# Weight splits in halves of 1024 columns instead of whole units of 2048, in a chain of two transformer models on one core

## The reference

```
first_block:  for i in 0, 1:
                  h = h + mixer_i(rmsnorm(h))        # 0: dilated windows, 24 heads; 1: block attention, 16 heads
                  h = h + square(relu(rmsnorm(h) @ w1)) @ w2            # w1 1024 x 4096, w2 4096 x 1024
second_block: h = layer_norm(16 meta tokens + x)                        # 272 rows
              for i in 0, 1:
                  u = h @ w_in                                          # 1024 x 3840
                  y_attn = sliding_window_attention(u) @ w_attn_proj
                  y_conv = silu(layer_norm(depthwise conv of 31 taps(u))) @ w_conv_proj
                  h = layer_norm(ALPHA*h + (sigmoid(ga)*y_attn + sigmoid(gc)*y_conv) @ w_out)
                  f = swiglu(h)  (i = 0)   or   mixture of 8 experts, 2 per token, each 1024 x 1408  (i = 1)
                  h = layer_norm(ALPHA*h + f)
```

## Time and profile before

| what | value |
|---|---|
| three executions | 1688.42, 1688.47, 1685.88 us; median 1688.42 |
| profiled execution | span 1685.1 us from first to last instruction; its own time is not listed apart |
| TensorE's granted clock | 0.987 of full speed on average |
| busy: PE, DVE, ACT, POOL | 97%, 73%, 57%, 19% of the span |

### The profile page before, as it was taken

The page is one execution under the profiler, slowest core; times in us unless marked ns, Lnnn a source line. Parts: engine busy times, 40 slices in busy tenths (PEclk is TensorE's granted clock), DMA queues, the critical chain, the costliest instruction groups (busy, mean ns, idle before and its releaser), DMA issues.

```text
span 1685.1 us, 27573 instructions
## 1 busy us (share of the span) xinstructions
PE 1639.9 (97%) x11042; PEld 1488.0 (88%) x11042; DVE 1238.1 (73%) x1760; ACT 966.9 (57%) x1374; POOL 322.1 (19%) x320
## 2 busy tenths in 40 slices
PE   8999999999989999999999999999899999999997
PEld 6988888898878889998899999999888888888886
DVE  6555666656557656898775554799788899888897
ACT  5556575446656734555454433555547777776775
POOL 2333553123325502143020001131020000000000
PEclk9999999999989999999999999999989999999999
DMA  7632455555234554543335454543328888888993
GB/s 295 230 110 91 150 191 188 183 204 185 101 124 177 195 183 181 184 150 119 134 124 200 175 175 175 167 151 128 149 75 322 343 338 344 332 336 331 352 346 127
DMA packets 50197, 339.76 MB, mean 202 GB/s; under 512 B 5575, under 2 KB 7839, under 8 KB 10351
## 3 DMA queue, kind: packets, MB, share of 16 engines
q1 hardware_dynamic: 47344, 328.79, 53.1%
q0 software_dynamic: 2720, 9.13, 1.7%
HBM read 336.76 MB, written 1.13 MB: 201 GB/s over the span
## 4 chain that ended last, share of the span: by engine, by line
PE 87%; DVE 6%; ACT 4%; issue 2%; POOL 1%; DMA 1%; SPq 0%; DVEq 0%; ACTq 0%; POOLq 0%
PE bank L509 12%; PE bank L483 8%; PE bank L485 8%; PE bank L484 8%; PE bank L507 7%; PE bank L927 5%; PE bank L928 5%; PE bank L929 5%; PE bank L640 3%; PE bank L642 3%; PE bank L641 3%; PE bank L960 2%; PE bank L959 2%; PE bank L958 2%; ACT wh L1165 1%
## 5 line engine op out<-in xcount | busy, mean ns | idle before, releaser
L1640 DVE TENSOR_TENSOR wl<-stg,wh 128x2048 fp32r<-128x2048 f32 x310 | 712.9, 2303 | 237.5 <-ACT wh L1165 235.3
L1165 ACT ACTIVATE wh<-stg 128x2048 fp32r<-128x2048 f32 x310 | 592.5, 1912 | 203.8 <-PE bank L929 85.2
L483 PE MATMUL bank<-xx,wh 128*128 128x272 f32 (+1 forms) x810 | 235.1, 290 | 1.1 <-DVE xx L2062 1.0
L485 PE MATMUL bank<-xx,wl 128*128 128x272 f32 (+1 forms) x810 | 232.5, 287 | 0.0
L484 PE MATMUL bank<-xx,wh 128*128 128x272 f32 (+1 forms) x810 | 232.3, 287 | 0.0
L509 PE MATMUL bank<-xx,wh 128*128 128x512 f32 x448 | 161.1, 398 | 0.0
L483 PEld LDWEIGHTS bank<-xx,wh 128*128 128x128 f32 x810 | 152.4, 188 | 3.0 <-issue 1.9
L484 PEld LDWEIGHTS bank<-xx,wh 128*128 128x128 f32 x810 | 153.6, 190 | 0.0
L485 PEld LDWEIGHTS bank<-xx,wl 128*128 128x128 f32 x810 | 152.4, 188 | 0.0
L509 PE MATMUL bank<-H,wh 128*128 128x512 f32 x434 | 151.3, 390 | 0.0
L927 PE MATMUL bank<-wh,GH 128*128 128x512 f32 (+3 forms) x400 | 147.6, 369 | 0.0
(11 more groups left out here) (366 smaller groups left out, 3526.8 us busy)
## 6 DMA issues: line engine op xcount, KB each, us to landing
stg<-in_w SPq DMA_DIRECT2D x310, 1024.0 KB, 4.8
BT<-bias_scratch POOLq DMA_DIRECT2D x3, 1024.0 KB, 11.4
BT<-bias_scratch POOLq DMA_DIRECT2D x1, 2048.0 KB, 13.0
BB<-bias_scratch POOLq DMA_DIRECT2D x2, 1024.0 KB, 6.5
res<-in_x SPq DMA_DIRECT2D x1, 1024.0 KB, 5.7
stg<-in_w SPq DMA_DIRECT2D x2, 512.0 KB, 6.8
BB<-bias_scratch POOLq DMA_DIRECT2D x2, 512.0 KB, 7.1
out<-res SPq DMA_DIRECT2D x4, 256.0 KB, 3.3
```

What stands on the lines that cost most here:

```text
L483: pe.matmul(out, wh, xh(kt), start=kt == 0, stop=False)
L485: ins = pe.matmul(out, wl, xh(kt), start=False, stop=kt == KT - 1)
L1165: act.activation(WH[u % NW][:, :], stg[u % NS][:, :], ACT.Copy).then_inc(*m.inc("w_high", u))
L1640: vec.tensor_tensor(WL[u % NW][:, :], stg[u % NS][:, :], WH[u % NW][:, :].bitcast(F32), ALU.subtract).then_inc(*m.inc("w_low_v", u))
```

## The change

Every split is made in halves v = 0 ... 621, of 1024 columns each, with an event of its own on each of the three engines: TensorE waits for the half it enters (`half_ready`) and gives back half by half, ScalarE's split of half v waits for TensorE's half v-6, VectorE's for ScalarE's half v. `enter(v)` puts down splits up to half v+5, at each half. The DMAs stay units of 1 MB and wait for the second half of unit u-4. `go_on` makes up for halves, and where a `one_ahead` stood outside the start it now adds one half. TensorE's matmuls and their order are the same.

```diff
+HU = UT // 2
+        def half_of(bufs, v):
+            return bufs[v // 2 % len(bufs)][:, v % 2 * HALF:(v % 2 + 1) * HALF]
...
-            def unit_ready(u):
-                w.wait_ge(*m.of("w_high", u))
-                w.wait_ge(*m.of("w_low_v", u))
+            def half_ready(v):
+                w.wait_ge(*m.of("w_high", v))
+                w.wait_ge(*m.of("w_low_v", v))
...
             def enter(self, u):
-                while self.made < min(u + NW, N_UNITS) and not self.held:
+                while self.made < min(u + 2 * NW, 2 * N_UNITS) and not self.held:
                     self.split(self.made)
                     self.made += 1
...
             def go_on(self):
                 self.held = False
-                self.enter((self.at - 1) // UT)
+                self.enter((self.at - 1) // HU)
...
-            def split(u):
-                w.wait_ge(*m.of(f"w_in{u % NS}", u))
-                if u >= NW:
-                    w.wait_ge(*m.of("group" if u - NW < EXPERT_UNIT else arm[0], ("unit", u - NW)))
-                act.activation(WH[u % NW][:, :], stg[u % NS][:, :], ACT.Copy).then_inc(*m.inc("w_high", u))
+            def split(v):
+                w.wait_ge(*(m.of("first_in") if v == 0 else m.of(f"w_in{v // 2 % NS}", v // 2)))
+                if v >= 2 * NW:
+                    w.wait_ge(*m.of("group" if v - 2 * NW < EXPERT_HALF else arm[0], ("half", v - 2 * NW)))
+                act.activation(half_of(WH, v), half_of(stg, v), ACT.Copy).then_inc(*m.inc("w_high", v))
...
-            def split(u):
-                w.wait_ge(*m.of("w_high", u))
-                vec.tensor_tensor(WL[u % NW][:, :], stg[u % NS][:, :], WH[u % NW][:, :].bitcast(F32),
-                                  ALU.subtract).then_inc(*m.inc("w_low_v", u))
+            def split(v):
+                w.wait_ge(*m.of("w_high", v))
+                vec.tensor_tensor(half_of(WL, v), half_of(stg, v), half_of(WH, v).bitcast(F32), ALU.subtract).then_inc(*m.inc("w_low_v", v))
...
-                    w.wait_ge(*m.of("w_high", u - NS))
-                    w.wait_ge(*m.of("w_low_v", u - NS))
+                    w.wait_ge(*m.of("w_high", 2 * (u - NS) + 1))
+                    w.wait_ge(*m.of("w_low_v", 2 * (u - NS) + 1))
```

More of the change, by code:

```diff
@@ L468, in gemm_lead @@
                             ins.then_inc(*m.inc("group", (name, nt)))
-                            if nt % 2:
-                                m.also("group", ("unit", u))
+                            m.also("group", ("half", 2 * u0 + nt))
                 at[0] += LEAD // 2 * UT
@@ L487, in gemm @@
                             ins.then_inc(*m.inc("group", (name, nt)))
[L488 to L491, removed]
+                            if half_over():
+                                m.also("group", ("half", at[0] // HU - 1))
+                        elif half_over():
+                            ins.then_inc(*m.inc("group", ("half", at[0] // HU - 1)))
                     if pump is not None:
@@ L644, in mixer @@
                                 ins.then_inc(*m.inc("group", ("qkv", l, gi, kind, tt)))
-                        if kt == KD - 1:
-                            m.also("group", ("unit", at[0] // UT - 1))
+                        if half_over():
+                            if kt < KD - 1:
+                                ins.then_inc(*m.inc("group", ("half", at[0] // HU - 1)))
+                            else:
+                                m.also("group", ("half", at[0] // HU - 1))
                         if (bi, kt) in plan:
@@ L682, in lead_tile @@
                             ins.then_inc(*m.inc("group", (name, nt)))
-                            if (base + nt * KT + kt + 1) % UT == 0:
-                                m.also("group", ("unit", u))
+                            if (base + nt * KT + kt + 1) % HU == 0:
+                                m.also("group", ("half", (base + nt * KT + kt) // HU))
                 for i in rest:
@@ L922, in gate_up @@
                                 for pi, (u, k, c, o) in enumerate(pieces):
-                                    if k == 0:
-                                        unit_ready(u)
+                                    for v in range(2 * u + k // HU, 2 * u + (k + c - 1) // HU + 1):
+                                        half_ready(v)
+                                    over = [v for v in (2 * u, 2 * u + 1) if i == nT - 1 and k < (v - 2 * u + 1) * HU <= k + c]
                                     wh, wl = WH[u % NW][:, k * P:(k + c) * P], WL[u % NW][:, k * P:(k + c) * P]
@@ L931, in gate_up @@
                                         ins.then_inc(*m.inc(f"group_{tag}", ("gu", x, gi, up, i)))
[L932 to L935, removed]
+                                        for v in over:
+                                            m.also(f"group_{tag}", ("half", v))
+                                    elif over:
+                                        ins.then_inc(*m.inc(f"group_{tag}", ("half", over[0])))
                             at[0] += nn
@@ L962, in down @@
                             ins.then_inc(*m.inc(f"group_{tag}", ("down", x, g, i)))
[L963 to L966, removed]
+                            if i == nT - 1 and half_over():
+                                m.also(f"group_{tag}", ("half", at[0] // HU - 1))
+                        elif i == nT - 1 and half_over():
+                            ins.then_inc(*m.inc(f"group_{tag}", ("half", at[0] // HU - 1)))
                 let_go(*sorted(held))
@@ L1746, in mixer @@
                     vec.tensor_scalar(dw_all, dw_all, 0.5, None, ALU.mult).then_inc(*m.inc("taps_scaled", 0))
-                    sp.one_ahead()
+                    for _ in range(2):
+                        sp.one_ahead()
                     w.wait_ge(*m.of("x_sq", st))
```

64 lines of the change are left out of this document (22 added, 42 removed).

## The result

Nine executions of the changed kernel have a median of 1690.29 us (1688.26 to 1691.66), nine of the kernel before 1686.33 us. The ratio is 1.0023, 95% interval 1.0014 to 1.0033: **slower, by about 4 us**. The prediction said 1686.7 us, a change of -1.7 us. The time lies within its range of 8 in 10 (1678.5 to 1695) and just above the forecast's own (1683 to 1690), and the direction does not agree with it. What came in kind is the slower one, by the catch-ups: it has the mixers at +2 and a new stretch at half clock behind n10.

The account below looks back on a forecast made before the run. TensorE was taken as the bound, busy 1639.9 of 1685.1 us, with both splitters waiting for it. Terms summed to -1.7 us, giving about 1686.7 us from the 1688.42 median; 8-in-10 range 1678.5 to 1695, forecast's own 1683 to 1690.

Parts of the forecast that it names:

- the slower one, by the catch-ups: Rival: three halves at both catch-ups, new half-clock stretch behind n10, mixers at +2; 1693 us middle, 1696 worst; chance 0.22.
- the mixers' term: Mixers 0 and 1: score jobs and copies stand behind halves instead of whole splits; -1.7 us in sum.
- -1.0 at 145: Mixers, TensorE's wait for Lm at 145.04: its maximum comes 1.05 us earlier, behind halves; -1.0 us.
- -0.7 at 166.40: Mixers, TensorE's 0.74 us wait for PTm, queued behind a ScalarE split: a half there is shorter; -0.7 us.
- +1.2 at n10: Catch-up at n10: three halves instead of one split before the norm's chain; TensorE's wait 1.74 to about 3.0 us.
- At the router +1.2: Catch-up before the router: the same exchange of one split for three halves, in the half-clock stretch; +1.2 us.
- Start -1.1: Kernel start: TensorE's 1.09 us wait at 17.95 for unit 1's low part goes; -1.1 us.
- Second convolution, gates and MH/ML together: Three halves replace two units before the gate, -0.6 us; shorter interruptions in the mix layers' MH/ML chains, -0.8 us.
- Experts -0.6: Expert stage: the 0.61 us wait at 1596.69, from a copy behind a ScalarE split, goes; -0.6 us.
- the rival by events: TensorE pays for 311 new events: +3.1 us upper bound, 1689.8 us; chance 0.04.
- VectorE as a bound: Rival: VectorE becomes the bound in some four convolution windows, about 1 us each; 1690.7 us; chance 0.07.
- Extra cost per unit: Chains VectorE paces, convolutions and norms with splits between: some ten units by 0.10 us; +1.0 us.

Follow-up runs that it names:

- e3: The changed kernel with both halves of a unit put down where the whole unit stood, in mixer 0 only; 1687.28 us, ratio 0.9997 to the kernel before.
- e6: e1, but from unit 1 on VectorE starts on a first half only when ScalarE has made both; 1688.66 us, ratio 1.0013 to the kernel before.
- e1: The changed kernel with both halves of each unit put down where the whole unit stood; 1682.17 us, ratio 0.9970 to the kernel before.
- e2: The changed kernel with two halves, not three, meant at both catch-ups; only the router's changed; 1689.78 us, ratio 1.0013 to the kernel before.
- e5: e1, but ScalarE's split of a half waits until TensorE has given back the whole unit three before; 1681.75 us, ratio 0.9974 to the kernel before.
- e8: The changed kernel with halves in pairs in mixer 0 and from the second model's first norm on; 1684.53 us, ratio 0.9984 to the kernel before.
- e4: The changed kernel with 34 unused matmuls in place of 22 in TensorE's wait behind n10; 1690.13 us, ratio 1.0017 to the kernel before.
- e7: e1 with 12 more unused matmuls in TensorE's wait behind n10; 1682.33 us, ratio 0.9975 to the kernel before.

## Why the prediction was wrong

**The step that failed is the mixers' term**, -1.7 us; the table has +3.6 - 1.4 - 0.1 in mixer 0 and -0.2 in mixer 1, together +1.9. It named the mechanism: the second score job stands behind exponential, ScalarE half and VectorE half in turn, 1.9 us later. Then it said "TensorE needs it later, and I reckon -0.5 there". That was reckoned for one block by following TensorE's present waits, and no row was read for when TensorE needs the second job once the first is no longer what it waits for. Measured: +3.6 us from 88 to 112, three blocks in a row, each handing its lateness to the next through bank and copy waits. e3 takes it away (-0.4), but pairs also bring the overlap back; e6, with the order of before and no overlap, has +0.5 there. So of the 4.0 us between the changed kernel and e1, 3.1 are the order and 0.9 the overlap. "Other steps have the same interleaving with nothing to gain: +0.5" hid the other two blocks.

Within the same term, -1.0 at 145 was near the number (-1.4) for another reason than the one given. No pair of halves followed ScalarE's there. A single half stands ahead of the job in place of a unit:

```profile
142.57 1.23 DVE L1622 TENSOR_TENSOR wl<-stg,wh 128x1024 fp32r<-128x1024 f32 x1 [2.50 <-ACT wh L1158]
143.71 0.55 DVE L1695 CUSTOM_DVE_ANT_1 xc<-bank,BT 128x384 f32<-128x384 f32 x1
```

and TensorE arrives there 3.6 us late, so that it has less to wait for. e1, where a pair does stand there and TensorE is not late, gains 0.8. -0.7 at 166.40 was a misreading. In the changed kernel the wait is the same 0.74:

```profile
168.50 0.32 PE L593 MATMUL bank<-sq,VT 128*64 128x128 f32 x1 [0.74 <-ACT PTm L1192]
...
167.57 0.87 ACT L1192 ACTIVATE PTm<-bank 128x512 f32<-128x512 f32 x2 [0.90 <-PE bank L577]
```

ScalarE was idle 0.90 us ahead of PTm, waiting for TensorE's own transposes. In the earlier trace rows PTm seemed queued behind the split because it started as the split ended; both causes ended together, and only one was looked at.

**The second step: the clock was held fixed.** The sum takes the stretches at 0.50 as they were and leaves them to the rivals. In the profiled executions the growth behind the load of x is +2.3 us, and +1.8 of it lies where a stretch changed its length: +1.5 behind mixer 0, -2.0 near 490, +1.5 behind n10, +0.8 behind the router. Without these places +0.5 is left where the forecast has -1.7, and this is the mixers' term, in part made good by others. In the medians the clock can weigh up to 4 us, as worked out above, more than in this pair of profiles. How the loss of 4 us divides between the two is not shown: a stretch does not cost half its length everywhere. e3 and e6 lack the one that the kernel before has behind mixer 0, and their growth there is +0.1 and -0.4 us.

**The catch-ups.** +1.2 at n10 was right to the digit (wait 1.74 to 2.94). The clock behind it was kept as a rival: a stretch of 3.4 us at 0.50, 1.5 us. It came with waits of 2.94 to 2.95 (changed, e2, e3) and with 1.89 or less in e1, e5 and e8 but not in e6, so the third half is not needed for it; filling the wait removes it (e4, e7). At the router +1.2 was forecast and +2.0 measured over 1236 to 1270: 1.2 up to the end of the longer wait, as forecast, and 0.8 behind it, in the longer stretch at 0.50.

**What was right.** Start -1.1 (-1.0). Second convolution, gates and MH/ML together -0.6 - 0.8 (-1.9). Experts -0.6 (-0.9). First convolution and its gates -0.3 (-0.1). TensorE's events 0: the drift between 195 and 375, 520 and 790, 880 and 1150, 1270 and 1590 is 0.0 to 0.1 us in each, so the added increments cost nothing that shows in these 1040 us. That also disposes of the rival by events. The Trainium skill (TensorE: Matmul & The Clock Gate, The cost: per-tile semaphore tail) has 26.3 ns for each of the increments that serialize at the end of tiles; for increments spread through a stream these traces do not bear it out. VectorE as a bound: no drift in the convolutions from 700 to 750, although it was busy there 49.88 of 50 us.

**Extra cost per unit.** Taken +1.0; e6 has +2, which its lower clock alone can explain, so the term is neither confirmed nor refuted. For the same 310 units ScalarE's splits take 57 us more (at most 50 was said) and VectorE's 38 (31 was said), nearly all of it in idle time.

**What the sum left out** is the one thing halves are good for: VectorE on the first half while ScalarE makes the second. It was named for DMAs and for 145, and priced nowhere as a whole. e1 against e6 makes it 6.5 to 7 us, some 2 of which can be the clock. The change forgoes most of it, by laying the halves apart: VectorE's idle time for ScalarE is 222.2 us there, 196.3 in e6 and 110.5 in e1. One more reading was off: the sum calls the thirteen MH/ML waits paced by VectorE, while nine of them end with ScalarE's MH; that MH waits for VectorE in turn (21.0 us in 12 waits), so nothing hangs on it.

Sum of the growths in the table: +0.8 (load of x, not the change's) -1.0 + 0.2 + 3.6 - 1.4 - 0.1 + 1.5 - 0.2 - 2.0 - 0.1 - 0.1 + 2.7 - 1.9 + 2.0 - 0.1 - 0.9 = +3.0. Of it +3.6 is the first three blocks of mixer 0, +1.5 behind 180 the longer stretch that follows it, and -2.0 near 490 a stretch of 10.2 us that shrank to 3.4.

## What to carry to other kernels

Splitting an instruction in two has two effects of opposite sign: the consumer engine can start on the first half, which needs the halves side by side, and the order of other work can be changed, by laying them apart. Here the first was worth 6.5 to 7 us (e1 against e6), and laying the halves apart cost 8 to 9 (the changed kernel against e1). The second figure contains most of the first, and both contain what the clock did, so they are not to be added. Before a piece of work for later is put between two jobs of a chain, look whether it waits for another engine that serves the same chain; if so, the chain pays both engines' turns though neither is full. And a median can move through the granted clock alone: compare its mean over all executions before a difference of some microseconds is put down to a place. An instruction that starts just as its predecessor ends is not thereby bound by it: ask what else released it at that moment.

## What the runs showed of the hardware

TensorE's stretches at 0.50 are not a property of the kernel alone. Executions of code that is identical up to there had, behind mixer 0, a stretch of 6.8 us (changed), 3.4 us (e2) and 6.8 us (e4), and e4 one at 104.9 and one at 401.8 that no other had. In these traces they last 3.4, 6.8, 10.2 or 13.7 us. A single profile can therefore owe some 1.5 us at a place to a stretch of 3.4 us more (2.0 and 2.3 us near 490, where 10.2 became 3.4); waits that repeat from trace to trace, like 0.74 at 166.40, are the safer reading. The kernels themselves differ in it too: means over all executions are 0.9889 (before), 0.9864 (changed), 0.9890 (e1), 0.9877 (e6). Filling TensorE's wait with unused matmuls removed a stretch twice at the same place (e4, e7), without a gain in the median that could be measured.
